# One inference step of a hybrid trunk with 64 experts: the sums and norms at the end stand inside the last unit's step, and the down weights are split one unit ahead into two buffers

## The reference, cut to what matters here

```python
w = take_along_axis(s, eidx); w = w / sum(w) * ROUTED_SCALE
hg = einsum('nd,edf->nef', x, w_gate)
hu = einsum('nd,edf->nef', x, w_up)
hid = silu(hg) * hu * combine[:, :, None]
y = einsum('nef,efd->nd', hid, w_down)          # w_down (64, 256, 1024)
sh = (silu(x @ w_sh_gate) * (x @ w_sh_up)) @ w_sh_down
h = h + gate2 * (y + sh)
y_out = h * rsqrt(mean(h*h) + EPS) * final_norm_g
```

## Time and profile before

| | us |
|---|---|
| three runs | 1106.01, 1113.50, 1113.51 |
| median | 1113.5 |
| the profiled execution | 1105.11 |
| its span | 1103.3 |
| TensorE matmul busy | 1046.7 (95%) |
| VectorE, ScalarE, GpSimd busy | 531.1, 355.2, 166.0 |

### The profile page before, as it was taken

How to read it: one execution, slowest core, us unless ns; L and a number is a source line. 1 busy time by engine, 2 the same in 40 slices (tenths; PEclk the granted TensorE clock), 3 DMA queues, 4 the chain that set the end, 5 groups by cost and what they waited for, 6 DMA issues and landing times.

```text
span 1103.3 us, 15100 instructions
## 1 busy us (share of the span) xinstructions
PE 1046.7 (95%) x4876; PEld 702.0 (64%) x4876; DVE 531.1 (48%) x1110; ACT 355.2 (32%) x476; POOL 166.0 (15%) x142
## 2 busy tenths in 40 slices
PE   4999999999899999999998999999999999999975
PEld 2489888788788897874645455555555555454532
DVE  2233544355698956944633434433344334333358
ACT  3333544326444445501322222222222222222101
POOL 0020232000000000000015222322322212111100
PEclk9999999999999999999999999999999999999998
DMA  9999777346555332740249999999999999999692
GB/s 354 395 293 356 114 117 106 136 175 213 202 185 184 116 117 96 240 160 0 97 195 409 383 405 399 416 412 398 415 415 417 410 404 418 416 408 383 243 405 109
DMA packets 88529, 306.62 MB, mean 278 GB/s; under 512 B 13398, under 2 KB 17750, under 8 KB 66464
## 3 DMA queue, kind: packets, MB, share of 16 engines
q1 hardware_dynamic: 68896, 270.63, 62.2%
q0 software_dynamic: 12256, 26.80, 10.5%
q10 hardware_dynamic: 7328, 8.55, 2.2%
HBM read 285.31 MB, written 36.85 MB: 292 GB/s over the span
## 4 chain that ended last, share of the span: by engine, by line
PE 60%; DVE 2%; issue 1%; ACT 1%; DVEq 0%
PE PS L2045 17%; PE PS L2047 8%; PE PS L2070 4%; PE PS L1944 4%; PE PS L2031 3%; PE PS L1691 3%; PE PS L2060 3%; PE PS L2062 2%; PE PS L2061 2%; PE PS L2002 1%; PE PS L2119 1%; PE PS L2086 1%; PE PS L1932 1%; PE PS L1933 1%; PE PS L1934 1%
## 5 line engine op out<-in xcount | busy, mean ns | idle before, releaser
L1098 POOL DMA_INDIRECT y_parts<-bigB,IDX x38 | 72.3, 1902 | 323.8 <-DVE bigB L1628 314.7
L2045 PE MATMUL PS<-bigB 128*128 128x512 f32 x224 | 102.3, 600 | 0.0
L1745 PE MATMUL PS<-bigB_r 128*128 128x384 f32 x288 | 98.6, 342 | 1.3 <-ACT bigB L790 1.3
L2047 PE MATMUL PS<-bigA,bigB 128*64 128x512 f32 x208 | 94.7, 598 | 3.3 <-issue 3.3
L1747 PE MATMUL PS<-bigB_r,bigA_r 128*128 128x384 f32 x288 | 96.5, 335 | 0.0
L1746 PE MATMUL PS<-nT_r,bigB_r 128*128 128x384 f32 x288 | 96.3, 334 | 0.0
L2048 PE MATMUL PS<-bigB 128*64 128x512 f32 x208 | 94.8, 598 | 0.0
L2045 PE MATMUL PS<-bigA,bigB 128*128 128x512 f32 x208 | 94.6, 597 | 0.0
L1628 DVE TENSOR_SCALAR bigB<-PS,bigD 128x1024 f32<-128x1024 f32 x40 | 51.3, 1284 | 89.2 <-PE PS L2062 55.0
L1237 DVE TENSOR_TENSOR bigA_r<-bigA,bigB_r 128x2048 fp32r<-128x2048 f32 x18 | 41.3, 2292 | 97.5 <-ACT bigB_r L816 97.5
L1594 DVE TENSOR_TENSOR bigB<-bigB,PS 128x256 f32<-128x256 f32 x40 | 16.9, 422 | 134.3 <-ACT bigB L989 134.3
(11 more groups left out here) (372 smaller groups left out, 2127.2 us busy)
## 6 DMA issues: line engine op xcount, KB each, us to landing
bigA<-in_w_in SPq DMA_DIRECT2D x17, 2048.0 KB, 11.0
bigB<-in_w_gate SPq DMA_DIRECT2D x27, 1024.0 KB, 11.0
bigB<-in_w_up SPq DMA_DIRECT2D x27, 1024.0 KB, 18.9
bigB<-in_w_down SPq DMA_DIRECT2D x27, 1024.0 KB, 19.0
bigA<-in_w_gate SPq DMA_DIRECT2D x26, 1024.0 KB, 8.2
bigA<-in_w_up SPq DMA_DIRECT2D x26, 1024.0 KB, 16.6
bigA<-in_w_down SPq DMA_DIRECT2D x26, 1024.0 KB, 19.2
bigA<-in_w_ada SPq DMA_DIRECT2D x8, 2048.0 KB, 10.0
```

What stands on the lines that cost most here:

```text
L1098: pool.indirect_dma_start(y_parts, bass.IndirectOffsetOnAxis(ap=IDX[:, p, 1:2], axis=0), YS[:, p % 2, :], None, bounds_check=T * TOPK - 1, ...
L1745: mm(out, wh, nh, start=(k == 0), stop=False)
L2045: last = mm(PS[:, 2 + b, :], XT[:, b, k, :], GU_W[s][:, :, k, :], start=first, stop=stop)
L2047: mm(PS[0:HALF, 2 + b, :], XT[:, b, k, 0:HALF], GU_W[2][:, :, k, :], start=first, stop=stop)
```

## The change

- The down weights of unit u are split one unit earlier: `down_high` and `down_low` of unit p + 1 stand in the step whose `down` belongs to unit p. On ScalarE the copy stands after the copy of the transposed hidden values and ahead of the silu; on VectorE the subtraction stands after `hidden_low` and ahead of `hidden`. Those of unit 0 stand ahead of the loop. `DNH` becomes two buffers, one for each slot, so the wait for the `down` before goes.
- What stood behind the loop on VectorE and TensorE now stands in the `Else` of each step, which runs for the last unit only. TensorE's `down` has a copy in both branches.
- In this last step VectorE builds the one-hots before the last `down` is done, adds three rows of the loaded parts (both of chunk 0, one of chunk 1) ahead of the last weighting, and does the rest behind it. TensorE adds the kept rows first. It takes chunk 3 of tile 0 (before: chunk 0) and chunks 2 and 3 of tile 2 (before: 0 and 1). So TensorE has 64 products behind the last weighting and VectorE two adds less; for tile 2 VectorE multiplies the gate into its own part early and into the part from PSUM at the end, with the norm of tile 1 between them.
- `OHT`, `ACC` and the last loaded part move to other places in memory.

The diff, with the moved bodies cut:

```diff
-        DNH = cut(bigC_r, 0, (2, D))
+        DNH = [cut(bigC_r, 0, (2, D)), cut(bigD_r, 0, (2, D))]
...
-            def down_high(turn, i, s):
+            def down_high(turn, s):
                 act.wait_ge(dn_loaded[s], 16 * turn)
-                if s == 0:
-                    act.wait_ge(sh_added, NT - 1)
-                else:
-                    act.wait_ge(dn_ready, i - 1)
-                nc.scalar.activation(DNH, DN_W[s], ACT.Copy).then_inc(dn_high, 1)
+                nc.scalar.activation(DNH[s], DN_W[s], ACT.Copy).then_inc(dn_high, 1)
+
+            act.wait_ge(sh_added, NT - 1)
+            down_high(1, 0)
 
             def step(i, p):
 
                 act.wait_ge(gu_ready, i)
-                if p % 3 < 2:
-                    down_high(pas * 4 + (p // 3 + 1), i, p % 3)
                 with act.If(i + 2 <= units):
                     take_xt(i + 1, p % 2)
                 act.wait_ge(ht_ready, i)
                 nc.scalar.activation((HTH if p % 3 < 2 else HT)[:, p % 2, :, :], PS[:, 5, 0:2 * P].rearrange("p (k t) -> p k t", k=2),
                                      ACT.Copy).then_inc(ht_done, 1)
                 with act.If(i + 1 <= units):
+                    if (p + 1) % 3 < 2:
+                        down_high(pas * 4 + ((p + 1) // 3 + 1), (p + 1) % 3)
                     act.wait_ge(hid_done, i)
                     silu(i, (1 + p) % 2)
...
-            def down_low(p):
-                if p % 3 < 2:
-                    dve.wait_ge(dn_high, pas * (BODY // 3 * 2) + (p // 3 * 2 + p % 3 + 1))
-                    nc.vector.tensor_tensor(DNL[p % 3], DN_W[p % 3], DNH.bitcast(F32), ALU.subtract).then_inc(dn_low, 1)
+            def down_low(nth, s):
+                dve.wait_ge(dn_high, nth)
+                nc.vector.tensor_tensor(DNL[s], DN_W[s], DNH[s].bitcast(F32), ALU.subtract).then_inc(dn_low, 1)
+
+            down_low(1, 0)
...
+            def last_sums():
+
+                dve.wait_ge(sh_added, NT)
+                one_row(0, 1, 1)
+                one_row(0, 2, 0)
+                one_row(0, 2, 1)
+                residual(0)
+                two_rows(1, 2)
+                one_row(1, 3, 0)
+                one_row(1, 3, 1)
+                final_norm(0)
+                residual(1)
+                m = 2
+                two_rows(m, 0)
+                one_row(m, 1, 0)
+                one_row(m, 1, 1)
+                link(nc.vector.tensor_tensor(ACC, ACC, gate(m), ALU.mult))
+                link(nc.vector.tensor_tensor(XH[:, m, :], XH[:, m, :], ACC, ALU.add))
+                final_norm(1)
+                dve.wait_ge(part_ready, m + 1)
+                link(nc.vector.tensor_tensor(two(ACC), PS[:, TAIL_BANK[m]:TAIL_BANK[m] + 2, :], two(gate(m)), ALU.mult))
+                nc.vector.tensor_tensor(XH[:, m, :], XH[:, m, :], ACC, ALU.add).then_inc(h2_done, 1)
+                dve.wait_ge(h2_done, m + 1)
+                final_norm(m)
+
+            def weigh(i, p):
+
+                dve.wait_ge(dn_ready, i)
+                dve.wait_ge(scat[p % 2], pas * (16 * BODY // 2) + (scat0 + 16 * (p // 2)))
+                nc.vector.tensor_scalar(YS[:, p % 2, :].rearrange("p (a n) -> p a n", a=2), PS[:, 6:8, :],
+                                        WC[:, p:p + 1], None, ALU.mult).then_inc(ys_done, 1)
+
+            in_loop = chain[0]
+
+            def step(i, p):
+
+                u = 1 + p + AHEAD
+                with dve.If(i + 1 <= units):
+                    one_hots(pas * 8 + u // 3 * 2, u % 3, u % 2)
+                    take_index(i + AHEAD, u % BODY, u % 3)
+                    hidden_low(i, p)
+                    if (p + 1) % 3 < 2:
+                        down_low(pas * (BODY // 3 * 2) + ((p + 1) // 3 * 2 + (p + 1) % 3 + 1), (p + 1) % 3)
+                    dve.wait_ge(ht_ready, i)
+                    hidden(i, (1 + p) % 2)
+                    nc.vector.tensor_copy(TOKF[:, p % 2:p % 2 + 1], IDX[:, p, 0:1])
+                    weigh(i, p)
+                with dve.Else():
+                    chain[0] = in_loop
+                    hidden_low(i, p)
+                    link(nc.vector.tensor_copy(TOKF[:, p % 2:p % 2 + 1], IDX[:, p, 0:1]))
+                    dve.wait_ge(ys_done, i)
+                    for b in range(2):
+                        for m in range(NT):
+                            ins = nc.vector.tensor_scalar(OHT[:, b, m, :], kc(K_R128), TOKF[:, b:b + 1], float(-P * m),
+                                                          ALU.subtract, ALU.is_equal)
+                    ins.then_inc(oht_done, 1)
+                    dve.wait_ge(xg_t, i)
+                    two_rows(0, 0)
+                    one_row(0, 1, 0)
+                    weigh(i, p)
+                    last_sums()
+
+            with dve.Fori(0, PASSES) as pas:
+                with dve.If(pas * BODY + 1 <= units):
+                    for p in range(BODY):
+                        i = pas * BODY + (1 + p)
+                        with dve.If(i <= units):
+                            step(i, p)
...
+            def last_sums(i):
+
+                pe.wait_ge(oht_done, 1)
+                pe.wait_ge(ys_done, i + 1)
+                kept_rows(0, True, False)
+                loaded_rows(0, 3, False, True).then_inc(part_ready, 1)
+                kept_rows(1, True, False)
+                loaded_rows(1, 0, False, False)
+                loaded_rows(1, 1, False, True).then_inc(part_ready, 1)
+                kept_rows(2, True, False)
+                loaded_rows(2, 2, False, False)
+                loaded_rows(2, 3, False, True).then_inc(part_ready, 1)
+
+            def finish_unit(i, p):
+
+                pe.wait_ge(ht_done, i)
+                pe.wait_ge(ys_done, i)
+                down(pas * 4 + (p // 3 + 1), p)
+
             def step(i, p):
 
                 with pe.If(i + 1 <= units):
@@ -2098,11 +2164,11 @@
                     hidden_t(i, p)
                     index(i + AHEAD, (1 + p + AHEAD) % 3, (1 + p + AHEAD) % 2)
                     gate_up(i, turn, 1 + p, range(4, KD))
+                    finish_unit(i, p)
                 with pe.Else():
                     hidden_t(i, p)
-                pe.wait_ge(ht_done, i)
-                pe.wait_ge(ys_done, i)
-                down(pas * 4 + (p // 3 + 1), p)
+                    finish_unit(i, p)
+                    last_sums(i)
```

115 lines of the change are left out of this document (33 added, 82 removed).

## The result

The changed kernel takes 1149.3 us in the median of 4 runs (1147.8 to 1153.7), the kernel before 1110.0 us in 4 runs beside it (1106.0 to 1113.5): a ratio of 1.036, 95% interval 1.031 to 1.042. The forecast was slower, and 1125 us, at most 1134. The direction was right and the size was not.

A forecast was written before the change was run, and what follows sets the result against it. A TensorE loop that ends transfer-bound: loop end +3.0, cheap branches would make the span +2.7, and TensorE's exit loads (9.5 x 2.5 us) take it from 1103.3 to 1115.0, +11.7. On the 1113.5 median: 1125 us, range 1108 to 1134.

The forecast's parts named there:

- What bounds the kernel: Expert loop: begins as a TensorE loop living on a stock of loaded weights, ends as a transfer loop, engines at 0.97.
- The silu behind the late load: End of the loop: a late down load now delays silu and `hidden`; last gate/up products end 7.0 us later.
- Does the transfer stream slip too?: Weight stream: slots return up to 7 us later, queued bytes keep engines busy, landings stay; cost zero, -2 to +3.
- The stock of loaded weights hides that: Loop start: the first subtraction delays VectorE's first one-hots by 2.3 us, hidden by the stock of loaded weights.
- What is given back: Last unit: both weight halves are ready, TensorE's 3.59 us stand goes; the loop ends 3.0 us later, not 7.0.
- The sums: Behind the last gate/up products: one-hots ready earlier, part reads 7.0 us later; VectorE's last operation at 1101.7, before 1100.2.
- The way out: Jumps over unused steps and passes, behind the sums: instruction loads of 2.5 us (TensorE, through at 1115.0) and 1.6 (VectorE, 1113.8).
- The jumps back after units 12, 24 and 36: Ends of loop passes: one instruction load each, all but about 1 us covered by the transfer-bound wait.
- Rival (c): Instruction loads at the exit cost 5.0 us each: TensorE through at 1138, +35, 1148 us; chance 0.06.
- Rival (a): Jumps at the exit stay cheap, the store keeps the larger loop or loads ahead: +2.7, 1116 us; chance 0.30.
- (b): Down loads are in time, so nothing moves before the last unit: -4.3, 1109 us with cheap jumps; chance 0.05.
- (d): Later release of slots starves the weight stream: +3 on top of any case; no separate chance given.

The follow-up runs named there:

- e_split_first_late: The split one unit ahead alone, sums behind the loop, first subtraction back in the first step, against the kernel before: 1110.4 us, ratio 1.000.
- e_split_only: The split one unit ahead into two buffers alone, sums behind the loop, against the kernel before: 1114.8 us, ratio 1.004.
- e_tail_only: The sums inside the last unit's step alone, the split at its old place with one buffer, against the kernel before: 1151.7 us, ratio 1.035.
- e_pad_pe: The kernel before with 42 never run matmuls in each of the twelve steps on TensorE: 1159.5 us, ratio 1.045.
- e_pad_dve_small: The kernel before with 4 never run operations in each of the twelve steps on VectorE: 1131.3 us, ratio 1.020.

## Why the prediction missed the size

- **What bounds the kernel: right.** TensorE and the transfers are both at their limit, so most of a stall of either is kept. The forecast didn't draw that conclusion for the stalls that it listed itself.
- **The silu behind the late load, "the last gate/up products end 7.0 us later": the size fits and the sign came, but the reason is not fully shown.** The loop without its start and its jumps back grew by 7.7 us, and from silu 0 to 39 `e_split_first_late` grew by 7.0. The sign that was named, more than nine waits of the copy for its load and late silus from about unit 10, came: 18 waits in the changed kernel, and late silus from unit 6 on. But taking the silu out from behind the copy did not give the time back, so that the size fits may in part be luck.
- **"Does the transfer stream slip too?" (forecast at no cost, from -2 to +3): not contradicted by the split, but the landings moved.** The down load of unit 37 landed at 1059.4 us and not at 1031.8. It was issued 29.6 us later (1036.1 and not 1006.5) and took less time, 23.3 us and not 25.3. So the lateness was handed to it by TensorE's stalls, which the forecast did not have. In `e_split_first_late` the copy of unit 37 starts behind its load at 1032.1 us, as before.
- **"The stock of loaded weights hides that" (the first subtraction): wrong.** The stock hides a late weight, but not a late one-hot column: in `e_split_only` and in the changed kernel TensorE waited 3.3 us for VectorE there, where it had waited 1.1, and the lower clock came on top. How much of the +5.3 us is the subtraction's is not known, since the old order takes 14.4 us at this place in three traces and 9.7 in the one that the ledger uses.
- **"What is given back": right.** Forecast -4.0 us, measured -3.6 (52.5 to 48.9 in the split alone).
- **The sums: right.** Forecast -5.5 us from the last gate/up products to the last operation, the split's share included; measured -4.5. The sums' own part is about -1: `e_tail_only` has 51.3 against 52.5. Behind the last weighting VectorE works almost without a gap: it waits 3.7 us for TensorE's first partial sum, which the forecast had at 3.4 (1068.6 to 1072.0), and 0.6 us once for a read. The reads were issued at 1085.1 us and not near 1054.6, for the loop had ended so much later.
- **The way out: right in kind, near in size.** TensorE: forecast 29.9 us (1085.1 to 1115.0), measured 31.4 (1118.75 to 1150.1), at 3.1 us for a jump where 2.5 was taken and a longer one of 4.7 at the top. VectorE: forecast 13.4, measured 19.6, with 2.1 to 2.7 us from branch to branch where a load of 1.6 and a branch of 0.26 were taken, and 3.7 at the top. It starts only behind the last operation and ends last, at 1151.5 us, where the forecast had TensorE last: +15.5 us instead of +10.2.
- **"The jumps back after units 12, 24 and 36 cost a load each as well; the transfer-bound wait covers all but about 1 us": this is the step that failed.** The forecast counted three loads, let a wait cover them, and left the 1 us that remained out of its sum. Measured: 22.2 us in the changed kernel, 24.0 in `e_tail_only`, which has no split. Each jump stops TensorE for 5.0 to 5.5 us and VectorE for 6.0 to 6.2. Where only TensorE's code was too large (`e_pad_pe`) the stop is 3.3 to 3.8 us, about that of a skipped step in the quiet tail (3.1 to 3.5), and where only VectorE's was, VectorE stops for 4.8; why it is longer with both is open. Then comes the lower clock, and then fewer transfers under way. The wait that was to cover the loads stood on ScalarE for the down weights; it covers what is late behind gate/up products, and nothing of a stop of TensorE itself.
- **Rival (c)**, dear loads of 5.0 us and 1148 us, came within 2 us of the measured 1149.3, and that is luck: it put all of it at the exit, where a load cost 3.1 us, and nothing at the jumps back. Rival (a) fell. (b) asked for down loads in time, which was not the case. Of (d), a stream starved by the later release of slots, the traces show 1 to 6 us of later issues behind 850 us in two kernels with the split alone.

The Trainium skill (Runtime: NRT & Kernel Launch, section Instruction fetch mechanics) says that a taken branch to a place outside the window of two loaded pages stalls until the page has been fetched. The traces agree that such stalls exist: 3.1 us a jump on TensorE's way out. It also says that prefetch is purely sequential and that there is "no instruction cache that benefits from spatial locality". Here they differ, and the measurement decides: the loop of the kernel before needed six loads on TensorE's queue in its first pass and none later, and its jump back over them cost nothing (11.8 to 12.0 us between the silus).

## What to carry to other kernels

Code in a loop can have a price even where it never runs. Before a rare branch is written out inside an unrolled loop, count the instruction loads of a steady pass for each engine: none means that the loop fits, and it may fit by little, on an engine that is far from busy (VectorE was 48% busy here). In this loop, which is at its limit on TensorE and on transfers, a stall cost more than the waiting row shows: 22.2 us of gaps for 15.6 us of TensorE's waits in the changed kernel, 13.1 for 7.2 in `e_pad_dve_small`, for the clock behind it. Where an early exit is needed, one jump was better here than one for each skipped step.
